# Column-strip sums for the 1024-row norms, collected conditioning rows and a rearranged order of steps in a two-block kernel on one Trainium2 core

## What is computed

```python
def first_block(x, ...):
    u = rmsnorm(h, norm_mix[l])                      # norm 0
    proj = u @ w_in[l]
    y_ssm = s5_branch(...)      # ends: y = gelu(y); y * sigmoid(y @ w_glu + b_glu)
    y_attn = stick_breaking_attention(q, k, v)       # 8 heads
    gates = sigmoid(u @ w_gate[l] + b_gate[l])
    merged = g_ssm * (y_ssm @ w_up_ssm[l]) + g_attn * (y_attn @ w_up_attn[l])
    h = h + merged @ w_out[l]
    hid = relu(rmsnorm(h, norm_mlp[l]) @ w_ff1[l])   # norm 1
    h = h + (hid * hid) @ w_ff2[l]
    return rmsnorm(h, norm_final)                    # norm 2

def hybrid_layer(x, c_act, ...):                     # twice, c_act = silu(c)
    ada = c_act @ w_ada + b_ada                      # 1024 -> 3072
    shift, scale, gate = split(ada, 3)
    u = x * (1.0 + scale) + shift
    proj = u @ w_in     # q_lat, kv_lat, k_rope, a, b and c inputs, gates, merge logits
    ...                 # convolutions, latent attention, merge
    out = m @ w_o
    return layer_norm(ALPHA * x + gate * out, ln_g, ln_b)   # mean l, var l
```

## Time and profile before

| | |
|---|---|
| median of 3 runs | 1056.01 us (1053.74 to 1057.05) |
| the profiled execution | 1058.53 us, span of the profile 1056.7 us |
| PE | busy 1011.7 us, 96% of the span |
| DVE | 696.7 us, 66% |
| ACT | 545.7 us, 52% |
| POOL | 375.9 us, 36% |
| granted clock of TensorE, mean | 0.984 of full |

### The profile page before, as it was taken

One profiled execution on the slowest core, in us unless ns is written; L12 is line 12 of the kernel. 1 busy time (PEld: TensorE's weight loads), 2 busy tenths in 40 slices (PEclk: granted clock), 3 DMA queues, 4 the chain that ended last, 5 costly groups with the idle time before them and its releaser, 6 DMA issues.

```text
span 1056.7 us, 19594 instructions
## 1 busy us (share of the span) xinstructions
PE 1011.7 (96%) x8132; PEld 957.7 (91%) x8132; DVE 696.7 (66%) x1052; ACT 545.7 (52%) x631; POOL 375.9 (36%) x159
## 2 busy tenths in 40 slices
PE   7998999989999999999999999999899999999996
PEld 6986887878999999989999999999699999999995
DVE  4959889786432222366878995865559789868563
ACT  5455565655544434457554745543466547446532
POOL 3079683003688887510066430000100566300000
PEclk8998999999999999999999999999899999999998
DMA  8652555766765665464744546553557354564601
GB/s 271 209 160 81 160 160 160 239 201 222 249 192 174 194 183 185 157 186 144 229 140 142 177 149 194 168 191 120 154 165 239 120 160 148 172 200 144 205 12 40
DMA packets 159496, 179.58 MB, mean 170 GB/s; under 512 B 5040, under 2 KB 141744, under 8 KB 159408
## 3 DMA queue, kind: packets, MB, share of 16 engines
q1 hardware_dynamic: 159024, 177.22, 53.3%
q0 software_dynamic: 384, 1.10, 0.3%
HBM read 177.26 MB, written 1.05 MB: 169 GB/s over the span
## 4 chain that ended last, share of the span: by engine, by line
PE 75%; DVE 11%; issue 7%; ACT 5%; DMA 1%; POOL 1%; SPq 0%; DVEq 0%; ACTq 0%; POOLq 0%
PE pg L1803 65%; DVE p_bu L1681 2%; PE p_s L1886 2%; DVE area L1246 2%; PE p_y L1957 1%; ACT w_hi L928 1%; ACT u_hi L903 1%; PE pg L1824 1%; PE p_s L1779 1%; DVE area L1264 1%; DVE rows L1288 1%; DVE area L1250 1%; PE p_s L1940 1%; DMA area<-in_c_state 1%; PE p_bu L1940 1%
## 5 line engine op out<-in xcount | busy, mean ns | idle before, releaser
L818 POOL TENSOR_TENSOR w_lo<-raw,w_hi 128x2048 fp32r<-128x2048 f32 x61 | 284.6, 4675 | 304.1 <-ACT w_hi L928 304.1
L928 ACT ACTIVATE w_hi<-raw 128x2048 fp32r<-128x2048 f32 (+3 forms) x153 | 275.1, 1804 | 68.3 <-PE pg L1803 30.7
L1803 PE MATMUL pg<-u_hi,w_hi 128*128 128x256 f32 x1536 | 213.7, 291 | 15.5 <-ACT u_hi L903 11.3
L1237 DVE TENSOR_TENSOR w_lo<-raw,w_hi 128x2048 fp32r<-128x2048 f32 (+2 forms) x92 | 190.5, 2083 | 54.6 <-ACT w_hi L928 54.4
L1803 PEld LDWEIGHTS pg<-u_hi,w_hi 128*128 128x128 f32 x1536 | 196.2, 194 | 26.0 <-issue 9.8
L1803 PE MATMUL pg<-u_lo,w_hi 128*128 128x256 f32 x1536 | 202.6, 285 | 0.0
L1803 PE MATMUL pg<-u_hi,w_lo 128*128 128x256 f32 x1536 | 200.2, 283 | 0.0
L1803 PEld LDWEIGHTS pg<-u_lo,w_hi 128*128 128x128 f32 x1536 | 193.9, 194 | 0.0
L1803 PEld LDWEIGHTS pg<-u_hi,w_lo 128*128 128x128 f32 x1536 | 191.4, 192 | 0.0
L934 ACT ACTIVATE area<-pg 128x512 f32<-128x512 f32 (+1 forms) x92 | 54.1, 588 | 155.2 <-PE pg L1803 143.3
L1681 DVE SCALAR_TENSOR_TENSOR p_bu<-area,par,p_bu 128x256 f32<-128x256 f32 x232 | 93.9, 483 | 0.9
(11 more groups left out here) (217 smaller groups left out, 1354.6 us busy)
## 6 DMA issues: line engine op xcount, KB each, us to landing
raw<-in_w_in SPq DMA_DIRECT2D x68, 1024.0 KB, 5.3
raw<-in_w_ff SPq DMA_DIRECT2D x32, 1024.0 KB, 5.6
raw<-in_w_ada SPq DMA_DIRECT2D x24, 1024.0 KB, 5.3
raw<-in_w_gate SPq DMA_DIRECT2D x8, 1024.0 KB, 7.8
raw<-in_w_o SPq DMA_DIRECT2D x8, 1024.0 KB, 5.2
raw<-in_w_out SPq DMA_DIRECT2D x4, 1024.0 KB, 7.0
raw<-in_w_b_out SPq DMA_DIRECT2D x4, 1024.0 KB, 5.0
raw<-in_w_c_out SPq DMA_DIRECT2D x4, 1024.0 KB, 5.2
```

The costliest lines, as they stand in the source:

```text
L818: pool.tensor_tensor(w_lo[:, s, 0:n], raw[:, r, 0:n], w_hi[:, s, 0:n].bitcast(F32), ALU.subtract).then_inc(sem(f"raw_free{r}"), 1)
L928: act.activation(dst, src, ACT.Copy).then_inc(*(c.event("w_hi", q["s"]) if i == len(parts) - 1 else c.step()))
L1237: ins = dve.tensor_tensor(dst, src, hi.bitcast(F32), ALU.subtract)
L1803: ins = pe.matmul(pg[g % 2][0:m, i * T:i * T + T], w[:, k, a:a + m], x[:, k, :], start=x is x_hi and w is wh and (i, k) == turns[0], stop= ...
```

## The change

- **Sums.** `STRIP = 32`. For every sum but norm 0's, the eight products use 32 columns of ones and go round four column strips of the PSUM bank `p_s` (columns T to 2T). ACT copies the four strips to `root`, and one product of PE with `pick` joins them and spreads the result to all partitions (`join_strips`). Then root and reciprocal as before.
- **Conditioning rows.** The products' weight is now 32 columns wide with silu_c in one of them (`selector`, a window into `mask2` or `odd_z`), so that panel after panel adds a row to the same strips. There are four parts of 9, 8, 3 and 4 panels; each part is copied once by ACT (`ada_rows`) and turned once by PE with two products of 32 columns (`ada_columns`). Part 0 stays in the bank of its group, parts 1 to 3 go to `p_z` and are no longer groups; their slot is freed by PE's last product. The 24 `ada_take` and 24 `ada_turn` go.
- **Start.** h is loaded by two queues, SP and ACT's; SP waits for its own half alone; the parameters' load on POOL waits for h's first; `mask2` is made later, on POOL (`ada_selector`). DVE does all eight rows of norm 0, then their lows, then w_lo.
- **Loop.** Six products that keep the clock stand before `stick_fails` of head 1; ACT's table for head 1 is preloaded.
- **Order.** The conditioning panels 11, 12 and 13 stand behind glu, before `glu_mul`, with up_ssm's first panel loaded between 11 and 12. The roots of the latents stand apart with a w_hi between and the sigmoid table ahead. The last gate take stands before a convolution step. At the boundary w_hi stands before the copy of the rows. `modulate` gives one of four pieces of u_hi to POOL.

The core of the diff:

```diff
-ADA_PARTS = ((0, 14), (14, 17), (17, 20), (20, 24))
+ADA_PARTS = ((0, 9), (9, 17), (17, 20), (20, 24))
...
+        step("join_strips", "norm", k)
         step("norm", k)
-        ada_panel(i)
-        step("ada_take", i)
-        ada_panel(i + 1)
-        step("ada_turn", i)
-        step("ada_take", i + 1)
-        ada_panel(i + 2)
-        step("ada_turn", i + 1)
+        for n in range(3):
+            ada_panel(i + n)
         step("modulate", key[1])
-        step("ada_take", i + 2)
+        step("ada_rows", part_of(i))
...
+        if m == 1:
+            step("keep_clock", 6, 1)
...
             ada_panel(10)
-            step("ada_turn", 9)
-            step("ada_take", 10)
         if m + 1 < HEADS:
             step("state", 2 * m + 1)
         if m in (2, 4):
             step("table", f + 1)
     step("stick_out", HEADS - 2)
-    step("ada_turn", 10)
+    step("ada_columns", 0)
...
     ada_panel(11)
-    step("ada_take", 11)
+    load("up_ssm", 0, 0)
+    ada_panel(12)
+    ada_panel(13)
     step("glu_mul")
     step("split", "yg")
-    ada_panel(12)
-    step("ada_turn", 11)
-    step("ada_take", 12)
     for n in range(2):
...
         step("u2_piece", j)
-    step("ada_take", 14)
+    step("join_strips", "norm", 1)
     step("norm", 1)
...
-        step("latent_roots", l)
+        step("latent_root", l, 0)
+        step("high_ahead", count["split"] + 3)
+        step("latent_root", l, 1)
+        step("table_set", "sigmoid_and_others")
...
+            if h == HEADS + 1:
+                step("gate_take", len(panels) - 1)
             if h in (3, 4):
...
-        step("gate_take", len(panels) - 1)
...
         step("ln_mean", l, 3)
+        step("join_strips", "mean", l)
         if l == LAYERS - 1:
             step("keep_clock", 8)
-        if l == 0:
-            step("ada_take", 20)
         step("ln_centre", l)
         if l == 0:
             ada_panel(21)
-            step("ada_turn", 20)
-            step("ada_take", 21)
+        step("ln_var", l)
+        step("join_strips", "var", l)
         step("ln", l)
         if l == 0:
             ada_panel(22)
-            step("ada_turn", 21)
-            step("ada_take", 22)
-            step("ada_turn", 22)
             ada_panel(23)
-        if l == 0:
             step("modulate", 1)
-            step("ada_take", 23)
+            step("high_ahead", count["split"] + 2)
+            step("ada_rows", 3)
...
-            return sem(f"raw_free{n}"), sum(p["split"] for p in PANELS[n:q["index"] + 1:RAW])
+            return sem(f"raw_free{n}"), sum(p["split"] or not p["groups"] for p in PANELS[n:q["index"] + 1:RAW])
...
+            def join_strips(a, b):
+                act.wait_ge(sem("strips"), over("strips", (a, b)))
+                past = [key for key in SUMS[:SUMS.index((a, b))] if key in ROOTS or key[0] == "lat"][-1]
+                act.wait_ge(sem("rstd"), over("rstd", ("lat_kv", past[1]) if past[0] == "lat" else past))
+                fn(root[:, 0, :], p_s[:, T:2 * T], ACT.Copy).then_inc(*c.event("strip_rows", (a, b)))
...
                         ins.then_inc(*(c.event("rows", "u0", j // 2) if j % 2 else c.step()))
-                        if j == 3:
-                            low_halves(first_splits(1, ahead))
-                        if j % 2 and j >= 3:
-                            low("u0", j // 2 - 1)
-                    low("u0", 3)
+                    for j in range(4):
+                        low("u0", j)
+                    low_halves(first_splits(1, ahead))
                 elif k == 2:
...
+                    if part == 0:
+                        pe.wait_ge(sem("selector"), over("selector"))
+                        group_start(g)
+                        rows = pg[g % 2]
...
                     w = slot(raw, q)
                     for k in range(KT):
-                        strip = slice(32 * (k % 4), 32 * (k % 4) + 32)
-                        ins = pe.matmul(pg[g % 2][strip, 0:256], silu_c[:, k:k + 1].broadcast_to([P, 32]), w[:, k, :], start=k < 4, stop=k >= KT - 4)
-                    ins.then_inc(sem("groups"), 1)
+                        strip = slice(STRIP * (k % 4), STRIP * (k % 4) + STRIP)
+                        ins = pe.matmul(rows[strip, 0:256], selector[part > 0][:, k, MIDDLE - row:MIDDLE - row + STRIP], w[:, k, :],
+                                        start=row == 0 and k < 4, stop=i == end - 1 and k >= KT - 4)
+                        if part == 0 and i < end - 1 and k == KT - 2:
+                            ins.then_inc(sem(f"bank_free{g % 2}"), 1)
+                    if part == 0:
+                        ins.then_inc(sem("groups"), 1)
+                    else:
+                        ins.then_inc(sem(f"raw_free{q['index'] % RAW}"), 1)
...
+                if SUMS.index(key):
+                    for i in (2 * j, 2 * j + 1):
+                        strip = slice(32 * (i % 4), 32 * (i % 4) + 32)
+                        ins = pe.matmul(p_s[strip, T:2 * T], ones[:, 0:32], src[:, i, :], start=i < 4, stop=i >= 4)
+                    if j == 3:
+                        ins.then_inc(*event("strips", key))
+                    return
...
+            def join_strips(a, b):
+                pe.wait_ge(sem("strip_rows"), over("strip_rows", (a, b)))
+                pe.matmul(p_s[:, 0:T], pick[:, 0:1].broadcast_to([P, P]), root[:, 0, :], start=True, stop=True).then_inc(*event("stats", (a, b)))
...
+            def ada_columns(part, _):
...
                 for j in range(2):
...
-                ins.then_inc(*event("ada_turned", i))
+                    ins = pe.matmul(p_c[:, STRIP * j:STRIP * j + STRIP], root[:, 1, P * j:P * j + P], pick[:, :], start=True, stop=True)
+                ins.then_inc(*event("ada_turned", part))
```

186 lines of the change are left out of this document (107 added, 79 removed).

## The result

The changed kernel is slower: a median of 1062.94 us (1062.35 to 1063.58, 5 executions) against 1054.09 us of the kernel before beside it (1051.77 to 1057.05), a ratio of 1.0079 [1.0062, 1.0097]. The prediction of 1053.3 is 9.6 us too low, and its range ends at 1061.0. The profiled execution took 1063.58 us, with a span of 1061.8.

The account below looks back on a forecast made before the run. The prediction took PE, busy 96% of the span, as the bound, with DVE and ACT pacing it in places. Its terms, from +9.2 behind glu to -4.8 for roots and gates, summed to -2.7: 1056.0 to 1053.3 us, range 1045.5 to 1061.

Parts of the forecast that it names:

- start, to head 1: Kernel start: norm 0's rows first on DVE let w_hi and w_lo come earlier, -1.9 us (-1.0 to -2.9).
- loop and tail: Loop over heads and just behind: turns and takes go, six products may keep the clock, -4.65 us (-3 to -6).
- glu wait: Behind the glu product: PE idles for up_ssm's second panel, whose slot ada 11 frees late, +9.2 us (7.5 to 10.5).
- clock behind it, up_ssm, out: After the glu idle: half clock costs +2.7 us; less PE work and a closed gap in up_ssm and out give -2.7.
- norm 1 and clock: Norm 1: the join waits for ACT's copy behind six u_hi, +2.25 us, and the clock falls, +1.8.
- ff1 turns, norm 2, q_lat: Two turns go in ff1, -1.0 us; fewer u_hi rows on ACT at norm 2 and q_lat, -1.0.
- roots and boundary: Latents' roots: early table load, -1.7 us; between the layers: w_hi first, a turn and half pieces gone, -2.4.
- gates: Hybrid layers' gates: moving the take ahead of DVE's convolution steps closes the 1.56 us gap twice, -3.1 us.
- the rest, to the end: The end: removed takes and turns are mostly off the path, selector steps cost nothing, -0.2 us (-0.9 to 0.6).
- Rival D: Sums: strips don't run side by side, so each sum costs as before plus a join, +3.4 us, 1056.7; chance 0.08.
- Rival B: New idles behind glu and at norm 1: the clock doesn't fall or costs nothing, -4.5 us, 1048.8; chance 0.25.
- Rival C: Glu, norm 1, layer boundary, loop: half clock costs its worst after each idle, 9.2 us more, 1062.5; chance 0.16.

Follow-up runs that it names:

- experiment 11: Kernel before with only the start's edits (h on two queues, norm 0's rows and lows ahead of w_lo): 1053.05 us, ratio 0.998.
- again: Kernel before, unedited, profiled a second time: median 1054.31 us, ratio 0.9999; profiled execution 1053.1, span 1051.3.
- experiment 3: Changed kernel with conditioning panel 13 drawing no weight split, so that up_ssm's w_hi stands behind va_hi: 1053.9 us, ratio 0.9997.
- experiment 13: Changed kernel with experiment 3's draw of splits, experiment 4's early join, experiment 6's gate take and rope_half one piece of out later: 1044.25 us, ratio 0.9907.
- experiment 2: Changed kernel with up_ssm's second panel also loaded ahead of conditioning panel 11: 1062.41 us, ratio 1.0071.
- experiment 4: Changed kernel with norm 1's join_strips behind the second u_hi piece instead of the fourth: 1060.69 us, ratio 1.0054.
- experiment 15: Experiment 13's kernel with the gate take forward again, merge1's second w_lo on DVE, and whole sums without joins: 1039.99 us, ratio 0.985.
- experiment 5: Changed kernel with all sums as whole products, without strips or joins: 1059.74 us, ratio 1.0051.
- Experiment 7: Kernel before with only each hybrid layer's last gate take moved ahead of the convolution step: 1058.9 us, ratio 1.0046.
- experiment 8: Changed kernel with the w_lo of merge1's second panel made by DVE instead of POOL: 1059.43 us, ratio 1.0041.
- Experiment 10: Kernel before with the six clock-keeping products put in before stick_fails of head 1: 1054.55 us, ratio 0.9998.
- experiments 9: Changed kernel without the six clock-keeping products before stick_fails of head 1: 1063.96 us, ratio 1.0097.
- experiment 6: Changed kernel with each hybrid layer's last gate take put back behind its convolution step: 1061.33 us, ratio 1.0072.

## Why the prediction was wrong

Three steps failed. The moved gate take was to gain 3.1 us and cost 1.9, since it made DVE wait for POOL. And most of the loop's 4.65 was read off the half clock of one execution; against the kernel of experiment 11, which has the same start, the loop is only 0.6 us shorter. And the difference, worked out against that slower execution, was put on a median that mostly lacks what it had lost.

In the table, the measured columns are differences of the changed kernel's trace to each of the two traces of the kernel before.

| term | predicted | to the first profile | to "again" |
|---|---|---|---|
| start, to head 1 | -1.9 | -3.3 | -5.4 |
| loop and tail | -4.65 | -4.4 | +1.4 |
| glu wait | +9.2 | +9.3 | +9.3 |
| clock behind it, up_ssm, out | 0.0 | +0.2 | +0.2 |
| norm 1 and clock | +4.05 | +3.9 | +3.9 |
| ff1 turns, norm 2, q_lat | -2.0 | -0.1 | +0.3 |
| roots and boundary | -4.1 | -3.1 | -1.8 |
| gates | -3.1 | +1.9 | +1.9 |
| the rest, to the end | -0.2 | +0.8 | +0.8 |
| sum | -2.7 | +5.1 | +10.5 |

**Right: the wait behind glu.** The term I trusted most came to +9.3, by the chain forecast, from the order of instructions and the durations of rows. The gap was 10.16, and the products behind it took 2.05 us for eight instead of 1.19. The clock's cost and what up_ssm and out save cancel, as forecast, but each is smaller than its 2.7: in experiment 3, at full clock there, up_ssm to the last sum of norm 1 takes 42.78 us against 44.55 and 44.39 before, so the clock cost 1.8 and the savings are 1.6. They would be larger without a wait of 2.61 us at 245.71, for squares that stand behind ACT's sines, which the forecast didn't have (experiment 13 removes it). Experiment 3 shows that the wait behind glu and its clock cost 9.0 in the median. What I had not seen is which of the two conditions was the cause: I named slot and load first, and experiment 2 shows that an earlier load alone shortens the gap by 1.6 us and the median by 0.5. The place of w_hi ahead of va_hi is the cause; the late load is only what it waits for.

**Right: norm 1**, +3.9 against +4.05, and the join behind six u_hi is shown as its cause (experiment 4: of the wait of 3.30, 1.01 is left). Rival D, that strips don't run side by side, is false: eight records take 0.64 us where nothing holds them. But the strips' joins cost more than the strips save, as whole sums show: 3.2 us with the late join, 2.0 in experiment 15 where that one was repaired. For the boundary I took the joins' hand-overs as 0.25 against half pieces of 0.86; there the two sums together are 0.9 us slower with strips (4.44 against 4.17, and 3.71 against 3.04, experiment 5).

**Wrong: the gates, -3.1, which came to +1.9.** This is the largest step that failed. The two gaps of 1.56 did go. My step "Next late would be PE itself" was wrong: next was DVE, in another place. The gate take ahead of DVE's convolution step lets PE and ACT go on sooner: ACT's next w_hi starts at 616.49, 6.5 us behind branch1 (609.95), where before it did so 8.4 behind (613.49 behind 605.13). So POOL is ready for its w_lo at 618.48, while DVE is still at `va_lo`. The rows fit a strict exchange, each waiting for the other's end, to a tenth (a w_lo of POOL takes 4.62 us in the median of the trace): POOL's w_lo ends at 623.67, and its own 4.62 us earlier is 619.05, the end of `va_lo`; DVE's w_lo, offered at 619.10, ends at 625.82, 2.15 us behind 623.67. In the kernel before DVE's w_lo was first, and POOL waited 0.96 of its 5.58 for it, where no one is waiting. DVE's convolution products, which have one operand in PSUM (L1708), were not slowed: the 88 that lie within a w_lo of POOL take 0.48 us each, as the other 144 do. Experiment 7 shows that this edit alone brings the 6.72, experiment 8 that it goes when POOL's step goes, and that the forecast gain is then there, 1.3 a layer of the 1.56 expected. The Trainium skill (SBUF — State Buffer, "Who interferes with whom") has the rule: a DVE instruction with two inputs in SBUF and a GpSimd instruction that reads SBUF share a port as an exclusive lock, and whoever is first keeps it for the whole instruction; the trace agrees, with 6.72 for 2.28 and with no loss where DVE's operand lies in PSUM. The prediction moved a step past w_lo's of two engines and didn't ask which of them would now be first.

**Wrong: the loop, by what the clock was taken for.** To the first profile the term comes out as forecast, -4.4 for -4.65, and that is luck: this execution had its half clock inside the loop. The loop's bound is DVE, as I had written. Its chain, from the first scan of the loop to the last rows that the tail needs, and the rest up to up_attn, in us:

| | before | again | experiment 11 | after |
|---|---|---|---|---|
| DVE's first scan starts | 82.69 | 82.92 | 78.56 | 79.37 |
| DVE's chain | 105.39 | 102.75 | 102.78 | 102.39 |
| from there to up_attn | 4.21 | 2.97 | 2.14 | 1.90 |

Experiment 10 has 102.76 and 2.14. So only the first profile has a longer chain, by 2.6 us, and that is what I had counted as 3.0. The turns that go give DVE 0.4 us, and behind it, where I had forecast 2.15, 2.3 us go against the first profile, 1.1 against "again" and 0.2 against experiment 11. The products that keep the clock changed neither median (experiments 9 and 10).

**Wrong: how the sum was put on the median.** I put the difference on 1056.0 as if the profiled execution's 2.5 us above it were spread over the whole kernel. But this execution starts head 2's gate panel at 106.98, where the three other traces with the old start do so at 103.33, 101.81 and 101.68 ("again", experiments 10 and 7). So I subtracted what it had lost there as a gain of the change, and started from a median of executions that lose less. The miss of 9.6 is made up so: the terms are 7.8 off against the first profile (the gates 5.0, ff1 to q_lat 1.9, roots and boundary 1.0, the end 1.0, the others, above all the start, -1.1 together), this step adds 2.5, and 0.6 goes since the changed kernel's profiled execution lies that much above its own median. Against "again" the loop's term alone is 6.0 off.

**ff1 to q_lat**, -0.1 for -2.0. The turns do go (12 records in 1.22 us became 4 in 0.36), but a gap of 0.80 at 299.15, which neither profile of the kernel before has, takes that back; the profile names nothing that it waits for.

**The start** did more than forecast in the traces: by DVE's first scan -3.3 and -3.6. All thirteen with the new start begin the first pass between 14.0 and 15.6 us and head 2's gate panel between 98.0 and 99.1; the four with the old one do so from 15.9 to 16.5 and from 101.7 to 107.0. The loads on two queues, for which I had put nothing, may have part in it; they were not run alone. In the median experiment 11 gained 0.7 us with an interval that reaches no change, and its two groups lie 4.1 us below and 1.6 above the kernel before beside it. What decides to which group an execution belongs isn't settled.

**The end**, +0.8: two joins on the path to the last root, where nothing else runs, for which I had put nothing.

**Rival B**, no fall of the clock behind the new idles, is out: it fell behind both.

**Rival C** had the right time (1062.5) by the wrong mechanism. The clock cost no more than was forecast; the loss came from DVE and POOL and from the profile chosen.

## What to carry to other kernels

When a step moves in a fixed order, list for each engine what is drawn ahead of the moved step and whose data it needs; an early weight split ahead of an activation split turned a late load into 9 us, and one number repaired it. When it moves past steps of DVE and POOL that both read two operands in SBUF, ask which will be ready first: who is second waits out the other's whole instruction. And profile the kernel before twice before building on a stretch at half clock: compare the same section in both, between cuts that both pass at full clock, and look at the engine that bounds the section.

## What the runs showed that was not expected

DVE and POOL shut each other out for the whole of a w_lo: 6.72 us for a step of 2.28, and on the other side 5.19 and 5.58 for one of 4.62.

The kernel before, unchanged, ran the loop in 105.55 us in one profiled execution and in 99.83 in another, with the granted clock at 0.50 and at 1.00 from 96 to 105 us, and at 1.00 and at 0.50 from 83 to 92. An idle of 2.25 us of PE stood ahead of the half clock in the first and one of 1.76, at 78.7, in the second; in the changed kernel an idle of 2.61 at 243.10 was followed by full clock:

```profile
247.00:257.00 10.00, 10.00 (x84) 9.46 (x83) 2.37 (x8) 4.81 (x5) 6.07 (x2) 1.00 0.35 105
```

In the kernel of experiment 6, whose steps up to there are the same, the same idle of 2.61 us (it ends at 246.46) was followed by half clock:

```profile
247.00:253.00 6.00, 6.00 (x31) 5.55 (x28) 0.45 (x2) 1.84 (x2) 4.58 (x1) 0.53 0.60 179
```

So the same idle at the same place lets the clock fall in one execution and not in another, and a term for the clock behind a gap of 2 to 3 us is a chance rather than a number.
